# Short convolution's projections in a hybrid encoder trunk: the input projection by one level of Strassen in 12 pairs, the output projection in the down projection's form

## Chip, cores, metric

One core of one Trainium2 chip. The metric is the device time of one execution in microseconds (us), the median of several runs. The engines are TensorE (PE, with its weight loads shown as PEld), VectorE (DVE), ScalarE (ACT), GpSimd (POOL) and SyncE (SP), which here issues all DMAs.

## What is computed

Two layers on x of 1024 tokens by 1024 features, float32. Layer 0 is differential attention, layer 1 a gated short convolution; each is followed by a gated ConvFFN, and a last RMSNorm ends it. The part that changes is the mixer of layer 1:

```python
h = rms_norm(x, conv_norm_g)                       # 1024 x 1024
b, c, u = split(h @ w_in, 3)                       # w_in 1024 x 3072
x = x + (b * dwconv3(c * u, conv_w)) @ w_out       # w_out 1024 x 1024, taps over 3 tokens
```

Around it stand `x + conv_ffn(rms_norm(x))` of layers 0 and 1: an up projection 1024 x 5632, a convolution over 3 tokens, silu(gate) * val, a down projection 2816 x 1024.

## The kernel before

Everything is kept transposed: features on the 128 partitions, 1024 tokens along the free axis. X is 8 tiles of 128 x 1024. A float32 operand is split in a high part (`fp32r`, by ACT's copy) and a low part (the difference, by POOL for weights, by DVE for data), and each product is three matmuls: high x high, high x low, low x high. Every matmul has 512 columns. The instruction streams are written out by hand for each engine and tied by semaphores; each engine runs its own queue in order.

**Dense jobs.** `full_job` (and `down` in `ffn`) makes one 128 x 1024 output tile in a PSUM slot from one weight tile of up to 8 input tiles: 48 matmuls, or 42 where a down chunk has 7 tiles. A weight tile passes through SP (`load_tile`, which waits until the job two before has ended), ACT (`split_hi`) and POOL (`split_lo`); there are two buffers. The order of weight tiles is T_QKV, T_WO, T_D0 (down 0), T_CIN, T_COUT, T_D1.

**Strassen up stage (`ffn`, first half).** The FFN's up projection runs as 22 pairs of output tiles (gate and value). Its 2 x 2 blocks are: input features in two halves (even and odd tiles), tokens in two halves. One level in Winograd's form takes 7 block products in place of 8: `up_product` does 4 x 3 = 12 matmuls for each, 84 a pair. The sums of the weights are POOL's (`up_sums`), their high parts ACT's (`up_hi`), their low parts POOL's (`up_lo`). The sums of the data (XB, four sets of 28 KB) are made once per stage. ACT copies three products out of PSUM (`copied`), DVE adds the results together (`c11`, `c22`, `c12`, `c21`), multiplies by the norm's factor (`normed`), and convolves (`taps`). The weights of pair p + 2 are loaded when pair p has used its own.

**What makes the operands.** While the last dense stage before an up stage runs (`dense(l, base, n)`: attention's output projection, and the conv mixer's), each finished X tile is added (DVE `x_add`, L1360), stored to DRAM (SP), spread and split for the up stage (ACT `spread`, L1023 to L1039; DVE `operands`, L1335 to L1350), squared in place (ACT, L1043) and summed (POOL `square_add`, L1638). In the same jobs POOL makes pair 0's weight sums (L1596 to L1614) and low parts (L1632, `first_lo`). XB's last set overlaps the operands of the running jobs; `y_head` says that their tiles there have been read for the last time, which is two input tiles before the last job's end. Pair 1's weights are loaded after the last job.

**Down stage (`ffn`, second half).** 24 jobs: 3 chunks (8, 7, 7 hidden tiles) by 8 output tiles, each added to X. Jobs 0 and 1 start interleaved while the hidden tiles come back from DRAM: 3 tiles of job 0, 3 of job 1, then 5 and 5. In the last chunk of down 0 `add_and_norm` and `norm_act` make XGh and XGl, the split normalized input of the conv mixer (L1320, L346).

**The conv mixer.** `conv_pair`: 24 `full_job`s with T_CIN's weights on XGh, XGl, three for each of 8 feature tiles (c, u, b). DVE multiplies by the norm's factor, forms c * u, two taps, times b, and the low part; ACT the middle tap and the high part. The result lies in Yh, Yl on chip. Then `dense(1, T_COUT, 3)`: 8 jobs on Yh, Yl.

Of the kernel before, what the change touches and what calls it, by code (L numbers as in the profile page):

```python
# [26 lines left out]
P = 128  # L27
# [34 lines left out]
T_CIN = T_D0 + len(CHUNKS) * KT  # L62
T_COUT = T_CIN + 3 * KT
# [6 lines left out]
KP = KT // 2  # L70
DMA_SCRATCH = 1024
# [9 lines left out]
def build(nc, x_in, positions, weights, ups, params_in, consts_in, lams_in, out):  # L81
    ctx = ExitStack()
    with ctx:
# [72 lines left out]
        h_at = [144, 152, 160] + [8 * t for t in range(18)] + [144]  # L156
        Hs = [at(f"H{t}", [P, 2, S], AR + w * K, F32R) for t, w in enumerate(h_at)]
        Hf = [at(f"Hf{t}", [P, S], AR + w * K + 4 * K) for t, w in enumerate(h_at)]
# [51 lines left out]
        def gcol(norm, kt):  # L210
# [17 lines left out]
        G = [dict(cp=sem(f"g{l}_copied"), t=sem(f"g{l}_t_made")) for l in range(2)]  # L228
# [19 lines left out]
        c_free, cu_made, ct_mid, ct_made = sem("conv_mm_free"), sem("cu_made"), sem("ct_mid"), sem("ct_made")  # L248
        cy_made, cyh, cyl, c_pad = sem("cy_made"), sem("cyh_made"), sem("cyl_made"), sem("conv_pad")
# [3 lines left out]
        per_layer = {"a": 8 * FT, "b": 8 * FT, "sums": 4 * FT, "hi": 2 * FT, "lo": 2 * FT, "mm": 7 * FT, "out": 3 * FT,  # L253
                     "ev": 4 * FT, "rn": 2 * FT, "mid": 2 * FT, "tap": 4 * FT, "silu": FT, "h": FT, "st": 8 * FT, "pad": 1,
                     "hh": FT, "hl": FT, "add": 2 * KT}
# [56 lines left out]
        def square_sum(pe, n):  # L312

            src = X[:, 0, :] if n in (1, 3) else acc[:, :]
# [41 lines left out]
        def norm_factor(act, n):  # L356
# [3 lines left out]
            dst = FR if n in (1, 3) else R  # L360
# [9 lines left out]
        def conv_col(ft, c):  # L370
            return par[:, bass.ds(ft * 3 + (C_CONV + c), 1)]
# [33 lines left out]
        def nth(l, k, count):  # L405

            return l * per_layer[k] + count
# [4 lines left out]
        def _(sp):  # L412
# [113 lines left out]
            def up_a(l, p):  # L526
                f, s = F, p % 2
                sp.dma_start(U1f[s][:, 1, 0:4:3, :], ups[l * FT + p, :, 0:2, :]).then_inc(f[f"a{s}"], 16)

            def up_b(l, p):  # L530
                f, s = F, p % 2
                sp.dma_start(U2f[s][:, 1, 1:3, :], ups[l * FT + p, :, 2:4, :]).then_inc(f[f"b{s}"], 16)

            def dense(l, base, n):
                for kt in range(KT):
                    if (0 if l else 1) <= kt < KT - 2:
                        load_tile(sp, base + kt + 2, kt % 2)
                    sp.wait_ge(N[n]["x"], kt + 1)
                    sp.dma_start(x_dram[kt], X[:, kt, :]).then_inc(x_st[kt], 16)
                    if kt == 1:  # L540
                        up_a(l, 0)
                        up_b(l, 0)
                up_a(l, 1)
                up_b(l, 1)

            def h_load(l, t):
                sp.dma_start(Hf[t][:, :], h_dram[t]).then_inc(h_in[t % 8], 16)
# [4 lines left out]
            def h_store(l, p):  # L552
                f = F
                sp.wait_ge(f["h"], nth(l, "h", p + 1))
                sp.dma_start(h_dram[p], Tv[:, :]).then_inc(f[f"st{p % 2}"], 16)

            def ffn(l, base, n):
                f = F
                for p in range(FT):
                    if p + 2 < FT:  # L560
                        sp.wait_ge(f["mm"], nth(l, "mm", 7 * p + 4))
                        up_a(l, p + 2)
                    if p == FT - 1:
                        sp.wait_ge(f["mm"], nth(l, "mm", 7 * (FT - 2) + 7))
                        sp.wait_ge(f["st0"], nth(l, "st", 16))
                        sp.wait_ge(f["st1"], nth(l, "st", 16))
                        h_load(l, 0)
                        h_load(l, 1)
                        sp.wait_ge(f["st0"], nth(l, "st", 32))
                        h_load(l, 2)  # L570
                    if p:
                        h_store(l, p - 1)
                    sp.wait_ge(f["mm"], nth(l, "mm", 7 * p + 7))
                    if p + 2 < FT:
                        up_b(l, p + 2)
# [5 lines left out]
                sp.wait_ge(f["st0"], nth(l, "st", 16 * (FT // 2)))  # L581
                for t in range(3, CHUNKS[0][1]):
                    h_load(l, t)
                for j in range(len(CHUNKS) * KT):
                    c, m = divmod(j, KT)
                    n2 = base + j + 2
                    if n2 < T_END:
                        load_tile(sp, n2, n2 % 2, down_cols(n2))
                    if j == 0:
                        h_store(l, FT - 1)  # L590
                    if j == 1:
                        sp.wait_ge(f["st1"], nth(l, "st", 16 * (FT // 2)))
                        for kt in range(1, KT):
                            x_load(kt)
                    if c + 1 < len(CHUNKS) and m < CHUNKS[c + 1][1] - CHUNKS[c + 1][0]:
                        h_load(l, CHUNKS[c + 1][0] + m)

            dense(0, T_WO, 1)
            ffn(0, T_D0, 1)
            for n in range(T_CIN, T_COUT):  # L600
                load_tile(sp, n + 2, n % 2)
            dense(1, T_COUT, 3)
            ffn(1, T_D1, 3)
# [10 lines left out]
        def _(pe):  # L614
# [124 lines left out]
            def dense(d, base):  # L739
                def one_of(n):  # L740
                    wait(pe, N[1 + 2 * d]["x"], n - 1)
                    full_job(pe, n + base, n % 2, n % 2, Yh, Yl, (cyh, cyl) if n == 0 else None, n == KT - 1,
                             d == 0 and n == 2)
                if d == 0:
                    for a in range(2):
                        dense_ahead(a, (KT - 1,))
                else:
                    one_of(0)
                    one_of(1)
                for n in range(2, KT):  # L750
                    one_of(n)

            dense(0, T_WO)


            def up_weight(p, o, kp):

                s, c = p % 2, slice(kp * P, (kp + 1) * P)
                if o < 4:
                    return U1[s][:, 0, o, c], U1[s][:, 1, o, c]  # L760
                if p == 0:
                    return U2h_first[:, o - 4, c], U2l_first[:, c] if o == O_S3 else U2[0][:, 1, o - 4, c]
                return U2[s][:, 0, o - 4, c], U2[s][:, 1, o - 4, c]

            def up_product(p, o, kps):
# [3 lines left out]
                for kp in kps:  # L769
                    wh, wl = up_weight(p, o, kp)  # L770
# [7 lines left out]
            def ffn(l, base, n):  # L778
                f, g = F, G[l]

                def first_pair():
                    early = (0, 1, 2)
                    pe.wait_ge(f["lo"], nth(l, "lo", 1))
                    pe.wait_ge(N[n]["x"], KT - 1)
                    for kp in early:
                        pe.wait_ge(N[n]["lo"], 2 * kp + 2)
                        up_product(0, O_A11, (kp,))
                    up_product(0, O_S1, early)
                    up_product(0, O_A12, early)
                    pe.wait_ge(N[n]["lo"], 2 * KP - 1)  # L790
                    up_product(0, O_A11, (3,)).then_inc(f["mm"], 1)
                    up_product(0, O_S1, (3,)).then_inc(f["mm"], 1)
                    pe.wait_ge(f["out"], nth(l, "out", 1))
                    up_product(0, O_S2, early)
                    pe.wait_ge(N[n]["lo"], 2 * KP)
                    up_product(0, O_S2, (3,)).then_inc(f["mm"], 1)
                    up_product(0, O_A12, (3,)).then_inc(f["mm"], 1)
                    pe.wait_ge(N[n]["lo"], 2 * KP + 1)

                def half_pair(p):  # L800
                    pe.wait_ge(f["lo"], nth(l, "lo", 2 * p + 1))
                    if p == 1:
                        pe.wait_ge(N[n]["x"], KT)
                    wait(pe, f["ev"], nth(l, "ev", 4 * p - 4))
                    up_product(p, O_A11, range(KP)).then_inc(f["mm"], 1)
                    pe.wait_ge(f["ev"], nth(l, "ev", 4 * p - 1))
# [937 lines left out]
```

## Time and profile before

| | |
|---|---|
| time, median of 3 runs | 2413.07 us (2411.49 to 2415.57) |
| the profiled execution | 2413.57 us, its span 2411.8 us |
| PE / PEld busy | 97% / 79% |
| DVE / ACT / POOL busy | 56% / 39% / 43% |
| matmuls | 10404 |
| mean granted TensorE clock | 0.993 |
| DMA | 239.49 MB, mean 99 GB/s |

Rows of the trace read as: start in us from the span's start, duration in us, engine, source line, operation, destination<-sources, shapes, how many were merged, and in brackets the engine's idle time before it and what released it. Busy spans of matmuls overlap (each is shown with 0.39 us, while one starts every 0.23 us), so pace is read from starts and counts. "L292" and "L773 to L775" are the lines of the helpers in which dense and Strassen matmuls are issued. SPq rows are the times of issue; landing is told by its own line.

### The profile page before, as it was taken

The page shows a single profiled execution, that of the slowest core. Times are in us where ns is not written, and L with a number is a line of the kernel's source. Part 1 is how long each engine was busy: PE and PEld are TensorE (multiplying, and loading weights), DVE is VectorE, ACT ScalarE, POOL GpSimd, SP SyncE. Part 2 cuts the span into 40 slices and gives each one's busy share as a digit, 9 for nine tenths or more (in the row PEclk, how much of TensorE's full clock was granted, in tenths as well). Part 3 has the DMA queues.
Part 4 walks back from the last instruction along what each step waited for, and adds up shares of the span by engine and source line. Part 5 has one row for each costly group of instructions (what it writes and reads, how often), then busy time and mean ns, then how long its engine had stood idle before and what let it go on. Part 6 is the DMA issues. An engine that isn't in the chain of part 4 may idle for free.

```text
span 2411.8 us, 26211 instructions
## 1 busy us (share of the span) xinstructions
PE 2337.6 (97%) x10404; PEld 1906.8 (79%) x10404; DVE 1350.4 (56%) x1240; ACT 941.9 (39%) x1069; POOL 1025.6 (43%) x661
## 2 busy tenths in 40 slices
PE   8899989999999999999999999999999999999997
PEld 6688767777777888888888888888778888888886
DVE  7566699999365555556422233335555555563223
ACT  5112178888445444444212211113444444442112
POOL 1112113333467776674222412123776667732221
PEclk9999999999999999999999999999999999999999
DMA  3553374351322222223422111113222222234222
GB/s 129 171 175 116 134 198 120 91 140 51 107 96 70 84 92 79 87 79 131 175 90 72 48 53 44 52 43 105 79 86 81 87 80 79 80 130 174 90 80 93
DMA packets 73808, 239.49 MB, mean 99 GB/s; under 512 B 8160, under 2 KB 8544, under 8 KB 73696
## 3 DMA queue, kind: packets, MB, share of 16 engines
q1 hardware_dynamic: 73696, 237.95, 30.3%
q8 instruction: 76, 1.25, 0.2%
q14 instruction: 36, 0.29, 0.0%
HBM read 177.10 MB, written 60.82 MB: 99 GB/s over the span
## 4 chain that ended last, share of the span: by engine, by line
PE 75%; issue 14%; DVE 5%; POOL 3%; ACT 3%; DMA 0%; POOLq 0%; SPq 0%; DVEq 0%; ACTq 0%
PE PS L292 36%; PE PS L773 11%; PE PS L775 11%; PE PS L774 11%; DVE nb L1288 2%; POOL Wst L277 2%; PE PS L685 1%; PE PS L663 1%; PE PS L671 1%; PE PS L664 1%; DVE X L1307 1%; ACT X L969 1%; POOL X L1638 1%; ACT X L981 1%; ACT At L976 1%
## 5 line engine op out<-in xcount | busy, mean ns | idle before, releaser
L277 POOL TENSOR_TENSOR Wst<-Wraw,Wst 128x1024 fp32r<-128x1024 f32 (+1 forms) x111 | 263.3, 2373 | 875.2 <-ACT Wst L271 875.1
L773 PE MATMUL PS<-XB,U 128*128 128x512 f32 x1208 | 472.2, 391 | 6.9 <-POOL U L1632 6.7
L775 PE MATMUL PS<-XB,U 128*128 128x512 f32 x1224 | 477.8, 390 | 0.0
L774 PE MATMUL PS<-XB,U 128*128 128x512 f32 x1208 | 471.7, 391 | 0.0
L292 PE MATMUL PS<-H,Wst 128*128 128x512 f32 x2070 | 470.1, 389 | 0.6 <-POOL Wst L277 0.4
L292 PEld LDWEIGHTS PS<-H,Wst 128*128 128x128 f32 x2070 | 388.3, 188 | 82.1 <-DVE Tv L1425 0.8
L292 PE MATMUL PS<-XGh,Wst 128*128 128x512 f32 x1536 | 419.6, 394 | 23.5 <-POOL Wst L277 12.5
L271 ACT ACTIVATE Wst<-Wraw 128x1024 fp32r<-128x1024 f32 (+1 forms) x111 | 114.0, 1029 | 649.1 <-DMA Wraw<-weights 649.0
L292 PEld LDWEIGHTS PS<-XGh,Wst 128*128 128x128 f32 x1536 | 289.6, 189 | 87.0 <-issue 23.6
L773 PEld LDWEIGHTS PS<-XB,U 128*128 128x128 f32 x1208 | 227.8, 189 | 55.7 <-POOL U L1632 7.6
L775 PEld LDWEIGHTS PS<-XB,U 128*128 128x128 f32 x1224 | 230.8, 189 | 48.5
L774 PEld LDWEIGHTS PS<-XB,U 128*128 128x128 f32 x1208 | 227.7, 189 | 47.3
L292 PE MATMUL PS<-XGl,Wst 128*128 128x512 f32 x768 | 238.9, 392 | 0.0
L1632 POOL TENSOR_TENSOR U<-U1f,U 128x2048 fp32r<-128x2048 f32 x44 | 203.3, 4621 | 7.1 <-ACT U L1049 0.9
L1084 ACT ACTIVATE PS<-rawg,par 128x1024 f32<-128x1024 f32 x44 | 53.2, 1210 | 389.1 <-DVE rawg L1406 389.1
L292 PEld LDWEIGHTS PS<-XGl,Wst 128*128 128x128 f32 x768 | 145.9, 190 | 30.9
L1288 DVE TENSOR_REDUCE nb<-PS 128x1 f32<-128x1024 f32 x128 | 154.0, 1210 | 8.9 <-PE PS L664 8.9
L1429 DVE TENSOR_TENSOR H<-Hf,H 128x1024 fp32r<-128x1024 f32 x44 | 71.5, 1626 | 138.9 <-ACT H L1093 138.5
L1632 POOL TENSOR_TENSOR U<-U2f,U 128x1536 fp32r<-128x1536 f32 x42 | 149.2, 3553 | 0.0
L1596 POOL TENSOR_TENSOR U1f<-U2f 128x512 f32<-128x512 f32 x44 | 57.9, 1315 | 210.1 <-DMA U2f<-ups 210.1
L292 PE MATMUL PS<-Yh,Wst 128*128 128x512 f32 x480 | 130.4, 390 | 0.5 <-POOL Wst L277 0.4
L1417 DVE SCALAR_TENSOR_TENSOR PS<-rawg,par,PS 128x1024 f32<-128x1024 f32 x88 | 113.4, 1289 | 28.6 <-ACT PS L1084 27.1
(185 smaller groups left out, 3192.1 us busy)
## 6 DMA issues: line engine op xcount, KB each, us to landing
Wraw<-weights SPq DMA_DIRECT2D x79, 512.0 KB, 3.5
U1f<-ups SPq DMA_DIRECT2D x44, 512.0 KB, 4.6
U2f<-ups SPq DMA_DIRECT2D x44, 512.0 KB, 3.7
h_scratch<-Tv SPq DMA_DIRECT2D x44, 512.0 KB, 5.4
Hf<-h_scratch SPq DMA_DIRECT2D x44, 512.0 KB, 4.4
Wraw<-weights SPq DMA_DIRECT2D x32, 448.0 KB, 3.2
x_scratch<-X SPq DMA_DIRECT2D x16, 512.0 KB, 3.5
X<-x_scratch SPq DMA_DIRECT2D x16, 512.0 KB, 7.5
```

Source lines behind the costliest of these rows:

```text
L271: act.activation(w[:, 0, 0:cols], raw[:, 0:cols], ACT.Copy).then_inc(w_hi, 1)
L277: pool.tensor_tensor(w[:, 1, 0:cols], raw[:, 0:cols], w[:, 0, 0:cols].bitcast(F32), ALU.subtract).then_inc(w_lo, 1)
L292: ins = pe.matmul(ps[:, h * HALF:(h + 1) * HALF], w, m[:, h * HALF:(h + 1) * HALF], start=begin, stop=last and w is wl)
L773: pe.matmul(ps, wh, bh, start=begin, stop=False, skip_group_check=True)
L774: pe.matmul(ps, wh, bl, start=False, stop=False, skip_group_check=True)
L775: ins = pe.matmul(ps, wl, bh, start=False, stop=kp == KP - 1, skip_group_check=True)
L1084: act.activation(conv_ps(kind), src[:, 1:S + 1], ACT.Identity, bias=ffn_col(l, p, kind, 3), scale=ffn_col(l, p, kind, 1)).then_inc(f["mid" ...
L1288: dve.tensor_reduce(nb[:, b:b + 1], slot(c), axis=AX_X, op=ALU.min).then_inc(nb_done, 1)
L1417: dve.scalar_tensor_tensor(out=T, in0=raw[:, off:off + S], scalar=ffn_col(l, p, kind, c), in1=T, op0=ALU.mult, op1=ALU.add).then_inc(f["ta ...
L1429: dve.tensor_tensor(Hs[t][:, 1, :], Hf[t][:, :], Hs[t][:, 0, :].bitcast(F32), ALU.subtract).then_inc(f["hl"], 1)
L1596: pool.tensor_tensor(U1f[s][:, 1, O_S1, :], U2f[s][:, 1, 1, :], U2f[s][:, 1, 2, :], ALU.add).then_inc(f["sums"], 1)
L1632: pool.tensor_tensor(u[s][:, 1, :, :], uf[s][:, 1, :, :], u[s][:, 0, :, :].bitcast(F32), ALU.subtract).then_inc(f["lo"], 1)
```

## The change

- The input projection runs in the up stage's form: weights repacked on the host (`_conv_pairs`) in 12 pairs, for each two feature tiles the pairs (c, u), (c', u'), (b, b'). PE's `ffn` is split into `up(g)` and `down(g, base)`; g = 0, 1, 2 are the FFN of layer 0, the conv mixer, the FFN of layer 1. T_CIN, `conv_pair`, XGh/XGl for this norm and their jobs are gone.
- So the last chunk of down 0 (8 jobs of 42 matmuls) becomes a maker of operands: `dense(CONV)` on all engines, where `MADE_BY` = (T_WO, T_D0 + 16, T_COUT) is the first job. `y_head` comes after the third of 7 tiles in its last job.
- A conv pair's DVE work: evacuation and norm as in the FFN; then for (c, u) the product and two taps in PSUM, for (b, b') the two products y. y tiles 0 to 5 go to DRAM (`y_store`) and come back; tiles 6 and 7 stay in Tv and Tg.
- The output projection starts in the down stage's form: `conv_out` has jobs 0 and 1 interleaved as 3, 3, 3, 3, 2 and 2 tiles, then six jobs of 8 tiles in the order `y_last`; `y_head` comes after the fourth of 8 tiles in the last one.
- X passes through DRAM once more: stored in `dense(CONV)`, X0 loaded in pair 1, X1 to X7 loaded after `cyl` = 8. SP then enters `dense(2)`, whose first instruction is the load of T_COUT + 2.
- Buffers move (`h_at`, `y_at`, `u_set`), so that the sets in use don't overlap.

The core of the diff (in this order: constants, the new `conv` of SP, `conv_out` of PE, `conv` of DVE):

```diff
-T_CIN = T_D0 + len(CHUNKS) * KT
-T_COUT = T_CIN + 3 * KT
+T_COUT = T_D0 + len(CHUNKS) * KT
+CPAIRS = 3 * KT // 2
+PAIRS = (FT, CPAIRS, FT)
+MADE_BY = (T_WO, T_D0 + 2 * KT, T_COUT)
...
+            def conv():
+                for p in range(CPAIRS):
+                    if p + 2 < CPAIRS:
+                        up_next(CONV, p)
+                    if p == CPAIRS - 1:
+                        sp.wait_ge(F["mm"], nth(CONV, "mm", 7 * (CPAIRS - 2) + 7))
+                        for t in range(2):
+                            sp.wait_ge(cy_st[t], 16 * (KT // 2 - 1))
+                        for t in range(3):
+                            y_load(t)
+                    if p + 2 < CPAIRS:
+                        up_next_rest(CONV, p)
+                    if p and p % 3 == 0:
+                        y_store(p // 3 - 1)
...
+                sp.wait_ge(F["mm"], nth(CONV, "mm", 7 * CPAIRS))
+                for t in range(3, KT - 2):
+                    y_load(t)
+                sp.wait_ge(cyl, KT)
+                for kt in range(1, KT):
+                    x_load(kt)
...
+            def conv_out():
...
+                pe.wait_ge(w_lo, T_COUT + 1)
+                pe.wait_ge(F["ev"], nth(CONV, "ev", 4 * CPAIRS - 1))
+                job(0, (0, 1, 2), True, False)
+                pe.wait_ge(w_lo, T_COUT + 2)
+                pe.wait_ge(F["ev"], nth(CONV, "ev", 4 * CPAIRS))
+                job(1, (0, 1, 2), True, False)
+                job(0, (3, 4, 5), False, False)
+                job(1, (3, 4, 5), False, False)
+                job(0, (6, 7), False, True).then_inc(tile_done, 1)
+                job(1, (6, 7), False, True).then_inc(tile_done, 1)
+                for j in range(2, KT):
+                    pe.wait_ge(w_lo, T_COUT + j + 1)
+                    wait(pe, N[3]["x"], j - 3)
+                    job(j, y_last, True, True).then_inc(tile_done, 1)
...
+                def convolved(p):
+                    k = p // 3 * 2 + p % 3
+                    normed(g, p)
...
+                    dve.tensor_tensor(rawg[:, 1:S + 1], rawg[:, 1:S + 1], rawv[:, 1:S + 1], ALU.mult).then_inc(cu_made, 1)
+                    T = conv_ps(p % 3)
...
+                        dve.scalar_tensor_tensor(out=T, in0=rawg[:, off:off + S], scalar=conv_col(k, tap), in1=T,
+                                                 op0=ALU.mult, op1=ALU.add).then_inc(ct_made, 1)
...
+                outputs(CPAIRS - 1)
+                for t in range(3, KT):
+                    y_lo(t)
```

## Rows read from the trace of the kernel before

**Rows 1.** The page's first part: busy us, share of span, instructions.

```profile
PE 2337.6 (97%) x10404; PEld 1906.8 (79%) x10404; DVE 1350.4 (56%) x1240; ACT 941.9 (39%) x1069; POOL 1025.6 (43%) x661
```

**Rows 2.** Busy time by stage: up 0, input projection, up 1; its header names the columns.

```profile
core 0: us, PE busy (x) PEld busy (x) DVE busy (x) ACT busy (x) POOL busy (x), PEclk, DMA share, GB/s
707.50:1134.70 427.20, 423.13 (x1853) 348.51 (x1852) 245.85 (x250) 188.66 (x186) 290.33 (x131) 1.00 0.27 87
...
1376.30:1639.30 263.00, 263.00 (x1156) 217.07 (x1157) 96.84 (x65) 45.88 (x44) 60.86 (x25) 1.00 0.14 48
...
1726.50:2154.90 428.40, 424.37 (x1853) 349.38 (x1853) 245.60 (x250) 188.48 (x186) 290.37 (x131) 0.99 0.27 86
```

**Rows 3.** Timeline, down 0: the X adds behind two neighbouring jobs of 42 matmuls.

```profile
1260.77 1.22 DVE L1460 TENSOR_TENSOR X<-PS,X 128x1024 f32<-128x1024 f32 x1 [1.82 <-PE PS L292]
...
1270.29 1.23 DVE L1460 TENSOR_TENSOR X<-PS,X 128x1024 f32<-128x1024 f32 x1 [1.93 <-PE PS L292]
```

**Rows 4.** Timeline, PE's first matmuls of the input projection.

```profile
1376.29 0.73 PE L292 MATMUL PS<-XGh,Wst 128*128 128x512 f32 x2 [1.32 <-DVE X L1320]
```

**Rows 5.** Pair 1 of up 0 by timeline, then stretches at half clock by windows.

```profile
733.12 0.50 PE L773 MATMUL PS<-XB,U 128*128 128x512 f32 x1 [3.37 <-POOL U L1632]
...
734.10:737.40 3.30, 3.30 (x9) 2.53 (x9) 3.30 (x2) 1.21 (x1) 3.30 (x1) 0.50 0.00 0
...
1752.20:1758.00 5.80, 5.80 (x14) 4.54 (x15) 5.80 (x3) 1.54 (x2) 5.80 (x2) 0.50 0.00 0
```

**Rows 6.** Timeline, DVE at the end of the output projection.

```profile
1725.27 2.65 DVE L1341 TENSOR_TENSOR XBf<-XBf 128x512 f32<-128x512 f32 x2 [3.50 <-ACT XBf L1023]
1727.84 1.21 DVE L1360 TENSOR_TENSOR X<-PS,X 128x1024 f32<-128x1024 f32 x1
```

**Rows 7.** Timeline, DVE and POOL in the output projection's jobs; a narrower split in down 0.

```profile
1683.05 1.22 DVE L1360 TENSOR_TENSOR X<-PS,X 128x1024 f32<-128x1024 f32 x1 [2.74 <-PE PS L292]
...
1690.99 4.18 POOL L1638 TENSOR_TENSOR X<-X 128x1024 f32<-128x1024 f32 x1 [0.77 <-ACT X L1043]
...
1701.15 3.36 POOL L277 TENSOR_TENSOR Wst<-Wraw,Wst 128x1024 fp32r<-128x1024 f32 x1
...
1704.81 1.23 DVE L1360 TENSOR_TENSOR X<-PS,X 128x1024 f32<-128x1024 f32 x1 [2.54 <-PE PS L292]
...
1706.84 4.61 POOL L1632 TENSOR_TENSOR U<-U1f,U 128x2048 fp32r<-128x2048 f32 x1
...
1707.26 4.75 DVE L1347 TENSOR_TENSOR XBf<-XBf 128x512 f32<-128x512 f32 x1 [1.22 <-ACT XBf L1023]
...
1711.41 2.84 POOL L277 TENSOR_TENSOR Wst<-Wraw,Wst 128x1024 fp32r<-128x1024 f32 x1
...
1284.37 2.12 POOL L277 TENSOR_TENSOR Wst<-Wraw,Wst 128x896 fp32r<-128x896 f32 x1 [7.66 <-ACT Wst L271]
```

**Rows 8.** The seam into down 0: timeline, loads by tile, the page's median.

```profile
1142.62 1.06 ACT L1093 ACTIVATE H<-Hf 128x1024 fp32r<-128x1024 f32 x1 [1.55 <-DMA Hf<-h_scratch]
...
1154.53 2.40 POOL L277 TENSOR_TENSOR Wst<-Wraw,Wst 128x1024 fp32r<-128x1024 f32 x1 [33.93 <-ACT Wst L271]
...
1157.08 1.16 PE L292 MATMUL PS<-H,Wst 128*128 128x512 f32 x4 [0.44 <-POOL Wst L277]
...
L550 SPq DMA_DIRECT2D X<-x_scratch x7: 320/440/1455, 1159.3 to 1163.3; - x7
...
DMA to landing us min/median/max: 5.7/8.1/9.6
...
L264 SPq DMA_DIRECT2D Wraw<-weights x1: 333/333/333, 1168.2 to 1168.2; - x1
...
DMA to landing us min/median/max: 7.0/7.0/7.0
...
Wraw<-weights SPq DMA_DIRECT2D x79, 512.0 KB, 3.5
```

**Rows 9.** Timeline, up 0: DVE ends pair 1, ACT copies S2's sum in pair 2.

```profile
754.12 0.69 DVE L1402 TENSOR_TENSOR rawv<-PS,FR 128x512 f32<-128x512 f32 x1 [2.03 <-PE PS L775]
...
762.68 0.58 ACT L1012 ACTIVATE sP<-PS 128x512 f32<-128x512 f32 x1
```

More of the change, by code:

```diff
@@ L736, in _, with wo, up_weight @@
             run_steps(step, 15)
[L739 to L749, printed above, removed]
-                for n in range(2, KT):
[L751 to L758, printed above, removed]
+            def wo():
+                for a in range(2):
+                    dense_ahead(a, (KT - 1,))
+                for n in range(2, KT):
+                    pe.wait_ge(N[1]["x"], n - 1)
+                    full_job(pe, n + T_WO, n % 2, n % 2, Yh, Yl, None, n == KT - 1, n == 2)
+            wo()
+            def up_weight(g, p, o, kp):
+                s, c = u_set(g, p), slice(kp * P, (kp + 1) * P)
                 if o < 4:
@@ L850, in ffn, with job @@
                     if j < 20:
-                        wait(pe, f["add"], nth(l, "add", j - 3))
+                        wait(pe, f["add"], nth(g, "add", j - 3))
                     else:
-                        pe.wait_ge(N[n + 1]["x"], j - 19)
-                    if l and j == len(CHUNKS) * KT - 1:
+                        pe.wait_ge(N[g + 2]["x"], j - 19)
+                    if g and j == len(CHUNKS) * KT - 1:
                         last_down(j, range(*CHUNKS[-1]))
                     else:
-                        down(j, range(*CHUNKS[j // KT]), True, True).then_inc(tile_done, 1)
+                        job(j, range(*CHUNKS[j // KT]), True, True).then_inc(tile_done, 1)
+            def conv_out():
+                def job(j, tiles, first, last):
+                    s = (T_COUT + j) % 2
+                    for t in tiles:
+                        if j < 2:
+                            pe.wait_ge(cyl, t + 1)
+                        k = slice(t * P, (t + 1) * P)
+                        ins = products(pe, down_slot(j), Wst[s][:, 0, k], Wst[s][:, 1, k], Ys[t][0][:, :], Ys[t][1][:, :],
+                                       first and t == tiles[0], last and t == tiles[-1])
+                        if j == KT - 1 and t == y_last[3]:
+                            ins.then_inc(y_head, 1)
+                    return ins
+                pe.wait_ge(w_lo, T_COUT + 1)
[12 more added lines that the diff above has]
+                    job(j, y_last, True, True).then_inc(tile_done, 1)
             def square_half(half):
@@ L877, in last_down @@
                 square_half(1)
[L879 to L898 removed]
+            up(0)
+            down(0, T_D0)
+            up(CONV)
+            conv_out()
+            up(2)
+            down(2, T_D1)
         @block.scalar
@@ L1398, in c21 @@
[L1398 to L1407 removed]
+                ins.then_inc(F["pad"], 1)
@@ L1505, in last_add @@
+            dense(0)
+            ffn(0, T_D0)
+            dense(CONV)
+            conv()
+            dense(2)
+            ffn(2, T_D1)
             def last_add(half):
```

736 lines of the change are left out of this document (402 added, 334 removed).

## Prediction

> **What bounds the kernel now.** First the page's table of busy time: TensorE is busy 97% of a 2411.8 us span [rows 1], so what the change is worth is the matmuls it takes away, less the new idle time it opens in TensorE's queue. Second, the table by stage [rows 2]. The short convolution's input projection is one stretch, 1376.3 to 1639.3: 263.0 us in which PE never rests, at full clock. The FFN up stage, whose form it is to take, stands there twice: 427.2 and 428.4 us. Third, the pace: two X adds, each released by a down job of 42 matmuls, start 9.52 us apart [rows 3], so one matmul costs 0.2267 us from start to start, 48 of them 10.88 us and a pair of 84 of them 19.04 us. Last, the seams, by the timeline, since the projection gets three new ones: the down stage into it [rows 4, 6, 7], its own first two pairs [rows 5], and it into its output projection [rows 8].
>
> The profiled execution took 2413.57 us (1.8 us around its span), 0.5 us over the median of 2413.07; the sum is made against 2413.57.
>
> **1. The products.** Removed are 24 jobs of 48 matmuls, 1152 in all: 263.0 us [rows 2], plus the 1.3 us that PE waits for the last X tile before the first of them [rows 4]. Added are 12 pairs of 84, 1008 matmuls: 228.5 us. An up stage costs more than its matmuls: 22 pairs are 1848 matmuls, 418.9 us, so the excess is 8.3 us in the first [rows 2] and 9.5 us in the second. It is made of the norm's sum on PE, small waits in pair 0, and one large wait: pair 1 starts 3.4 us late, since its weight tiles can be loaded only when the job before has ended, and then comes a stretch at half clock [rows 5]. That stretch held 9 matmuls in 3.3 us in one stage and 14 in 5.8 us in the other; at full pace they take 2.0 and 3.2 us, so it cost 1.3 to 2.6 us. All this depends on the first two pairs, and the conv stage has the same code there, so it pays it once: I take the middle, 8.9 us. New stage 237.4 us, old 264.3: -26.9 us.
>
> The ten further pairs I cost at their matmuls alone. Their cover: DVE does less than in an FFN pair (one product and two taps in place of four taps and a gate), ACT less too, POOL the same. The tightest link is ACT's copy of S2's sum, which PE needs before the fifth product. In the FFN the pair that begins when c21 of the one before is read at 754.12 has it copied at 763.26 [rows 9], 9.3 us in, and needs it four products (10.9 us) in: slack 1.6 us. The queue ahead of it is shorter in the conv stage, so 0.
>
> **2. The last chunk of down 0 becomes the maker of the operands.** Its eight jobs now carry what the jobs of the output projection carry today: x_add, spread, the operand sums, squares, x stores, and on POOL the sums and the low parts of pair 0's weights. There a job lasts 10.88 us, here 9.52. Who pays is POOL's queue, since split_lo of the next weight tile stands in it. Measure from the end of job 3, whose X add starts at 1683.05 [rows 7]. POOL adds squares from 1690.99, makes four sums to 1701.15, and only then splits tile 6, to 1704.51: 21.5 us after that X add. Job 5's end, when tile 6 is needed, has its X add at 1704.81, 21.76 us after: a slack of next to nothing. In the new cadence the need comes at 19.04 us. The split is of 896 columns, 2.12 us instead of 2.40 [rows 7], which gives back 0.3. PE waits about 21.2 - 19.0 = 2.2 us. The next tile (1711.41 + 2.84, 31.2 us after, needed at 28.6 + 2.2 = 30.8, 0.3 to 0.6 less for the narrower splits) is then just in time. I take +2.2; bounds 0 (POOL's work moves with the jobs) and +5 (the second wait opens too). No clock loss is added: the wait of 1.3 us in [rows 4] was followed by none.
>
> DVE in that chain took 4.75 us for an operation of 128x512, a size that elsewhere takes it 0.69 [rows 9], while POOL ran 4.61 us of low parts [rows 7]. The Trainium skill, page "SBUF — State Buffer", section "Who interferes with whom", says that a DVE operation with two SBUF inputs and a GpSimd one that reads SBUF exclude each other, the loser waiting for the whole instruction. By that rule the tighter cadence could put one more DVE operation ahead of POOL's split; by the row of the two differences, 2.65 us [rows 6], this wait would then be 4.9 us and the sum 2398.8 us. The rows themselves carry 2.2; the bound of +5 holds the other.
>
> **3. The kt = 7 step of both later seams.** Tile 6's spread waits for y_head, which today comes 12 matmuls before the end of the last job; the change puts it 24 before. Today the add of X tile 7 starts at 1727.84, held behind DVE's two differences of tile 6 [rows 6], although PE was done at 1726.5 [rows 2]. With those differences earlier it can start at 1726.7. Everything to pair 1's weights hangs on it. So -1.1 us in the conv stage and -1.1 in the second FFN: -2.2 us. Bounds 0 and -2.2.
>
> **4. Into the output projection.** Before, PE passed from one to the other with no idle time. Now take the end of the last pair as zero. PE runs jobs 0 and 1 as 3, 3, 3, 3, 2, 2 tiles: job 0 ends at 84 matmuls = 19.0 us, job 1 at 21.8. Operand tiles 3 to 5 are loaded only after the last pair; in the down seam the third of these landed at 1142.6 [rows 8], 7.9 us after the pair's end at 1134.7 [rows 2]. Then ACT 1.06 [rows 8], DVE 1.22 as for an X add of that size [rows 7]: tile 5 is ready at 10.3, needed at 10.9, no wait. DVE's low parts of tiles 6 and 7 follow to 12.7. SP waits for exactly that (cyl = 8), and then issues seven X loads of 512 KB. Seven such loads landed 5.7 to 9.6 us after issue [rows 8], the first at 1165.0 and the last at 1172.8, so one behind another they come 1.3 us apart. Here the first lands near 16.2 (12.9 and the 3.5 us of a lone load, less 0.2), the seventh near 24.0.
> Behind them on SP's queue stands the load of weight tile 2, which waits for job 0's end: issued at 19.2, it lands behind the X loads at 25.3 (6.1 us later; the same tile behind X loads took 7.0 in the down seam, 3.5 is the median [rows 8]). ACT's split 1.06, POOL's 2.40, handovers 0.2: 29.0. PE has nothing from 21.8 on: 7.2 us idle. Who waits behind it: DVE, for job 2, and ACT's next spread behind the split; both catch up within the stage. The down seam hides the same chain since its job 1 has 30 matmuls left when the load goes out, and still waited 0.4 us [rows 8]; here 12 are left, 4.1 us less cover, and the X loads come earlier. The clock falls after such a wait; between 1.3 and 2.6 us [rows 5], I take 2.2, as the wait is longer. +9.4 us. Bounds: 4.6 + 1.3 = 5.9 if the load isn't held by the X loads; 13 if the low parts end 2 us later.
>
> **Sum.** -26.9 + 2.2 - 2.2 + 9.4 = -17.5 us: 2413.57 - 17.5 = **2396.1 us**.
>
> **Rivals.**
> A. The seams are covered: the weight load isn't held (5.9 in place of 9.4) and POOL follows its jobs (0 in place of 2.2). -26.9 - 2.2 + 5.9 = -23.2: 2390.4 us. For it: the transfers fill at most 0.27 of the DMA engines' time in these stages [rows 2]. Against: tile 6's split has no slack even today [rows 7].
> B. The chains pile up: 5 us in the last chunk, 13 at the output projection, nothing gained in part 3: -26.9 + 18 = -8.9: 2404.7 us.
> C. Slower than before. One mechanism: from pair 2 on the weight tiles land late, so POOL's sums, ACT's high part and, queued behind it, the copy of S2's sum come late in each pair. The slack is 1.6 us [rows 9]. The 17.5 us are used up over 10 pairs at 1.75 us each, that is when loads land 3.35 us later than in the FFN; at 4.5 us later the pairs cost +29 us: 2425.1 us. For it: SP's queue has new y stores in it. Against: they come after the next weight load in the queue, three times in the stage, while the FFN stores a tile in every pair.
> D. It does what it says and nothing else: 144 fewer matmuls, -32.6 us, 2381 us. The seams would have to be free, and those of [rows 5] aren't.
>
> **How the numbers follow.** Forecast 2396.1: 0.55. A: 0.20. B: 0.16. C: 0.05. D: 0.04. The likeliest case alone reaches from 2393 to 2399; for 8 in 10 the range takes in A and most of B: 2388 to 2404. A measurement can tell 0.2% (4.8 us) from no change. Faster by more than that means under 2408.7: all but C and a tail of B, 0.92; within it 0.03; slower 0.05.
>
> **What would show it.** By stage: the conv up stage near 236 us with about 1013 matmuls, one wait of PE on POOL's U near 3.4 us; one wait of PE on POOL's Wst of about 2 us before job 6 of down 0's last chunk; one of about 7 us before the third job of the output projection, its Wraw load landing about 6 us after issue, with a stretch at half clock behind it. Wrong would be: waits of PE inside pairs 2 to 11; no wait at the output projection; a last chunk that waits at every job.

## The result, and the profile after

The changed kernel takes 2399.84 us (median of 5 runs, 2398.33 to 2403.92), the kernel before 2413.97 us beside it (5 runs, 2411.49 to 2415.89). The ratio is 0.9944, with 95% between 0.9933 and 0.9955: faster by 13.5 us by the ratio and by 14.1 by the medians, where 17.5 were forecast (2396.1 us, range 2388 to 2404). The profiled execution took 2399.84 us with a span of 2398.0, against 2413.57 and 2411.8 before, so the traces have 13.8 us to explain.

The page of the changed kernel, its table of busy time, the clock by slices and the transfers. The row of rows 1 is answered by the first:

```profile
PE 2311.8 (96%) x10260; PEld 1884.2 (79%) x10260; DVE 1401.9 (58%) x1311; ACT 991.5 (41%) x1116; POOL 1138.8 (47%) x711
...
PEclk9999999999999999999999999999999999999998
...
U1f<-ups SPq DMA_DIRECT2D x56, 512.0 KB, 4.5
U2f<-ups SPq DMA_DIRECT2D x56, 512.0 KB, 3.8
Wraw<-weights SPq DMA_DIRECT2D x55, 512.0 KB, 4.1
...
X<-x_scratch SPq DMA_DIRECT2D x24, 512.0 KB, 7.3
```

There are 144 matmuls fewer than in [rows 1], as the diff says. The weight tiles of the dense jobs (Wraw) take a median of 4.1 us to land where they took 3.5 [rows 8], but the 24 of the old input projection are no longer among them. The pairs' weight tiles (U1f, U2f) take 4.5 and 3.8 us; before it was 4.6 and 3.7.

Where the time went is told by stage. Busy time of the changed kernel by stage: up 0, down 0, the input projection, its output projection; then four short stretches in which the granted clock was 0.50 (up 1 took 427.3 us):

```profile
core 0: us, PE busy (x) PEld busy (x) DVE busy (x) ACT busy (x) POOL busy (x), PEclk, DMA share, GB/s
709.10:1137.30 428.20, 424.12 (x1854) 349.38 (x1853) 245.39 (x250) 188.37 (x186) 290.01 (x131) 0.99 0.27 86
1137.30:1380.90 243.60, 241.48 (x1057) 199.21 (x1056) 105.98 (x73) 72.66 (x68) 79.63 (x35) 0.99 0.34 121
1380.90:1619.00 238.10, 234.06 (x1014) 191.81 (x1013) 107.46 (x113) 80.55 (x80) 160.36 (x71) 0.99 0.23 78
1619.00:1714.80 95.80, 89.38 (x385) 73.39 (x384) 56.90 (x41) 39.33 (x35) 46.18 (x19) 0.96 0.37 137
...
1361.50:1364.90 3.40, 3.40 (x10) 2.62 (x9) 3.40 (x2) 0.95 (x1) 3.40 (x2) 0.50 0.24 98
1647.40:1651.60 4.20, 4.20 (x10) 3.33 (x11) 2.98 (x4) 2.08 (x2) 0.00 (x0) 0.50 0.32 116
...
1405.90:1412.60 6.70, 6.07 (x14) 4.81 (x15) 6.67 (x3) 0.64 (x2) 6.67 (x3) 0.50 0.04 15
...
733.40:740.20 6.80, 5.54 (x13) 4.38 (x14) 6.80 (x4) 1.99 (x3) 6.80 (x3) 0.50 0.11 44
```

The input projection took 263.0 us [rows 2] and takes 238.1. The stages' starts and ends of before stand in [rows 2] too: up 0 went from 427.2 to 428.2, down 0 (1134.7 to 1376.3, 241.6 us) to 243.6, the output projection (1639.3 to 1726.5, 87.2 us) to 95.8, up 1 from 428.4 to 427.3. Up 0 starts 1.6 us later, at 709.1, although no line ahead of it has changed its work. What follows up 1 takes 1.0 us less. In all: +1.6 +1.0 +2.0 -24.9 +8.6 -1.1 -1.0 = -13.8 us.

What PE waited for in the changed kernel, from 640 us on, summed by releaser (total us, times, longest):

```profile
PE PS L306 <- POOL Wst L291: 11.2, 5, 6.4
PE PS L830 <- POOL U L1764: 10.1, 3, 3.4
PE PS L830 <- ACT sP L1088: 2.2, 4, 0.6
```

The U waits are the three second pairs, where there were two [rows 5]. Between 1410 and 1619, pairs 2 to 11 of the input projection, PE waits for nothing. The Wst waits lie one at each place where a weight tile is split late: the forecast's two are these, by PE's timeline (in brackets the idle time and its releaser):

```profile
1360.12 1.20 PE L306 MATMUL PS<-H,Wst 128*128 128x512 f32 x4 [1.81 <-POOL Wst L291]
...
1647.33 1.22 PE L306 MATMUL PS<-Y,Wst 128*128 128x512 f32 x2 [6.42 <-POOL Wst L291]
```

The bracket counts from the drawn end of the last matmul; by starts and pace the gaps are 2.0 and 6.6 us, which is how the forecast reckoned. The first stands before job 6 of down 0's last chunk, the second before the output projection's third job. A third, of 2.2 us near 687, is in attention's output projection, which the diff doesn't change and where before had none.

### The profile page after: what moved, and what is told of

Its sections match the earlier page's. It is cut to its first block, busy times and chain, and to the rows that moved or that the text cites. A ratio compares the mean times of both kernels' runs of the same rounds, so it can differ in the third digit from the quotient of the medians.

```text
span 2398.0 us, 26048 instructions
## 1 busy us (share of the span) xinstructions
PE 2311.8 (96%) x10260; PEld 1884.2 (79%) x10260; DVE 1401.9 (58%) x1311; ACT 991.5 (41%) x1116; POOL 1138.8 (47%) x711
## 4 chain that ended last, share of the span: by engine, by line
PE 72%; issue 14%; DVE 5%; POOL 5%; ACT 3%; DMA 1%; POOLq 0%; DVEq 0%; ACTq 0%
PE PS L306 24%; PE PS L830 14%; PE PS L831 14%; PE PS L832 14%; DVE nb L1393 2%; POOL Wst L291 2%; PE PS L749 1%; PE PS L727 1%; PE PS L735 1%; POOL X L1771 1%; PE PS L728 1%; DVE X L1412 1%; ACT X L1045 1%; DMA Wraw<-weights 1%; ACT X L1057 1%
## 5 line engine op out<-in xcount | busy, mean ns | idle before, releaser
L830 PE MATMUL PS<-XB,U 128*128 128x512 f32 x1532 | 599.8, 392 | 10.6 <-POOL U L1764 10.1
L832 PE MATMUL PS<-XB,U 128*128 128x512 f32 x1556 | 607.8, 391 | 0.0
L831 PE MATMUL PS<-XB,U 128*128 128x512 f32 x1532 | 598.6, 391 | 0.0
L291 POOL TENSOR_TENSOR Wst<-Wraw,Wst 128x1024 fp32r<-128x1024 f32 (+1 forms) x87 | 208.2, 2395 | 673.3 <-ACT Wst L285 673.3
L830 PEld LDWEIGHTS PS<-XB,U 128*128 128x128 f32 x1532 | 289.3, 189 | 73.2 <-POOL U L1764 11.4
L832 PEld LDWEIGHTS PS<-XB,U 128*128 128x128 f32 x1556 | 293.7, 189 | 61.6
L831 PEld LDWEIGHTS PS<-XB,U 128*128 128x128 f32 x1532 | 289.5, 189 | 60.0
L1764 POOL TENSOR_TENSOR U<-U1f,U 128x2048 fp32r<-128x2048 f32 x56 | 259.5, 4635 | 8.6 <-ACT U L1125 1.0
L306 PE MATMUL PS<-XGh,Wst 128*128 128x512 f32 x768 | 212.7, 396 | 22.5 <-POOL Wst L291 13.3
L1764 POOL TENSOR_TENSOR U<-U2f,U 128x1536 fp32r<-128x1536 f32 x53 | 188.7, 3560 | 0.0
L306 PEld LDWEIGHTS PS<-XGh,Wst 128*128 128x128 f32 x768 | 145.6, 191 | 54.4 <-issue 23.1
L1088 ACT ACTIVATE sP<-PS 128x512 f32<-128x512 f32 x168 | 98.3, 587 | 168.2 <-PE PS L832 168.2
L1125 ACT ACTIVATE U<-U1f 128x2048 fp32r<-128x2048 f32 x56 | 107.4, 1918 | 47.8 <-POOL U1f L1732 47.8
L306 PE MATMUL PS<-XGl,Wst 128*128 128x512 f32 x384 | 120.1, 394 | 0.0
```

The costliest lines, as they stand in the source:

```text
L291: pool.tensor_tensor(w[:, 1, 0:cols], raw[:, 0:cols], w[:, 0, 0:cols].bitcast(F32), ALU.subtract).then_inc(w_lo, 1)
L306: ins = pe.matmul(ps[:, h * HALF:(h + 1) * HALF], w, m[:, h * HALF:(h + 1) * HALF], start=begin, stop=last and w is wl)
L830: pe.matmul(ps, wh, bh, start=begin, stop=False, skip_group_check=True)
L831: pe.matmul(ps, wh, bl, start=False, stop=False, skip_group_check=True)
L832: ins = pe.matmul(ps, wl, bh, start=False, stop=kp == KP - 1, skip_group_check=True)
L1088: act.activation(dst[:, :], bank(p, role), ACT.Copy).then_inc(F["out"], 1)
```

## The experiments

Each is the changed kernel with one edit unless said otherwise. Ratios are to the kernel before, run beside it. The theory going in is the forecast's: every late microsecond sits at a seam, where POOL's or SP's queue delivers a weight tile late; the pairs themselves are free. The rivals were that the wait at the output projection comes from PE's order of jobs or from the clock alone, that POOL's wait moves with the jobs, and that the stages which cost more in unchanged code are slowed by the change.

**e1_xlate: the X loads out of the weight load's way.**

```
                 sp.wait_ge(cyl, KT)
-                for kt in range(1, KT):
-                    x_load(kt)
+                x_load(1)
...
                         load_tile(sp, base + kt + 2, kt % 2, down_cols(base + kt + 2))
+                    if g == 2 and kt == 0:
+                        for late in range(2, KT):
+                            x_load(late)
```

> Only the order of SP's queue changes: X1 is still loaded ahead, X2 to X7 after the output projection's weight tile 2. Theory (that load is held by the X loads ahead of it: 5.56 us to land): it lands in 3.6 us, PE's wait before job 2 falls from 6.4 to about 4.5 us, the kernel is 2 us faster than the changed one (about 2397.5 at its median). Rival (the wait is set by the late end of job 0 alone and the queue costs nothing): wait 6.4, no change. Rival 2: X2 to X7 land too late and job 3 waits instead: no gain.

Measured: 2399.23 us, ratio 0.9942 [0.9925, 0.9958]. The load of weight tile 2 in e1_xlate, its time to land (min/median/max), and PE's wait in the output projection:

```profile
DMA to landing us min/median/max: 3.6/3.6/3.6
...
PE PS L306 <- POOL Wst L291: 4.5, 1, 4.5
```

In the changed kernel the same load took 5.6 us, and the wait was 6.4. So 2.0 us of the wait were the seven X loads in front. The other 4.5 us are a lone load and two splits behind 12 matmuls. That is the lower bound the forecast had given (4.6). The stage gave back 1.1 us of them (94.7 us against 95.8): in e1_xlate 15 matmuls ran at half clock behind the wait, in 6.2 us, in place of 10 in 4.2, which costs 0.9 us more. The medians differ by 0.6 us, too little to tell from none, where 2 were expected.

**e2_order: more matmuls between the first job's end and the third's start.**

```
-                job(0, (3, 4, 5), False, False)
-                job(1, (3, 4, 5), False, False)
-                job(0, (6, 7), False, True).then_inc(tile_done, 1)
-                job(1, (6, 7), False, True).then_inc(tile_done, 1)
+                job(0, (3, 4, 5, 6, 7), False, True).then_inc(tile_done, 1)
+                job(1, (3, 4, 5, 6, 7), False, True).then_inc(tile_done, 1)
```

> Only the order of the first two output jobs changes: 3, 3, 5, 5 tiles in place of 3, 3, 3, 3, 2, 2, so that job 0 ends 4.1 us earlier and weight tile 2 is issued 4.1 us earlier. Theory: the seven X loads are still ahead of it in the queue and end at the same time, so the tile lands at the same place (some 24 us behind the last pair), takes about 9 us from issue, and PE waits 6 to 6.4 us as before: within 1 us of the changed kernel. Rival (cover is all that lacks): the wait falls to 2.3 us, 4 us faster plus the clock's 1.9.

Measured: 2400.35 us, ratio 0.9941 [0.9925, 0.9958]. The same load and wait in e2_order:

```profile
L278 SPq DMA_DIRECT2D Wraw<-weights x1: 333/333/333, 1632.8 to 1632.8; - x1
...
DMA to landing us min/median/max: 11.0/11.0/11.0
...
PE PS L306 <- POOL Wst L291: 7.8, 1, 7.8
```

The tile goes out sooner, right behind the seven X loads (issued from 1629.1 to 1632.1), and takes 11.0 us to land: PE's order alone gives nothing, because the load is then held longer. The wait was expected to stay at 6 to 6.4 us and grew to 7.8. Counted from the start of the stage the tile lands at 26.2 us, in the changed kernel at 24.8; 0.5 of this is that the X loads go out 0.5 us later, the rest has no cause found.

**e3_both: the two edits together.**

> Both of the former edits. Theory (two causes in series, each hidden by the other): tile 2 is issued at 15.2 us behind the last pair, lands at 18.8, is split by 22.4; PE waits under 1 us and the clock does not fall: 5.7 + 1.9 = 7.6 us faster than the changed kernel, about 2392 us, more than the sum of the two edits alone. If they add up only: 2 to 3 us. If the low parts of y tiles 6 and 7 are late, PE waits inside job 0 instead.

Measured: 2397.51 us, ratio 0.9932 [0.9915, 0.9948]. Its output projection by the table of stages, its waits there, and the load of weight tile 3:

```profile
1615.90:1708.90 93.00, 88.19 (x386) 71.74 (x385) 61.63 (x41) 39.28 (x35) 46.92 (x19) 1.00 0.39 141
...
PE PS L306 <- POOL Wst L291: 4.8, 4, 2.2
...
DMA to landing us min/median/max: 8.7/8.7/8.7
```

The stage falls by 2.8 us and the median by 2.3, not by 7.6. Tile 2 did as expected: it landed in 3.9 us, and PE waited 0.7 for it. But the one wait of 6.4 has become four of at most 2.2: the six X loads now stand before tile 3, which takes 8.7 us to land (PE waits 1.4 us), and before job 6 the split of its tile waits in POOL's queue (2.2 us), as in down 0. So moving one load hands the wait on to the next item of the queues; e7_best below, which spreads the X loads and moves POOL's sums too, takes most of it away. The stretch at half clock is gone (clock 1.00 over the stage).

**e4_sums: POOL's sums one job earlier.**

```
-                    if kt == 3:
+                    if kt == 2:
                         up_sums(g, 0, 0)
                         first_sums(g)
```

> One number changes: POOL makes the weight sums of pair 0 in job 2 of each of the three operand-making stages in place of job 3. Theory (POOL's queue holds back the split of weight tile 6): the waits of PE before job 6 vanish, about 2.0 us in the last chunk of down 0 with the 1.7 us of half clock behind it, and 2.4 us in the attention's output projection: 4 to 6 us faster than the changed kernel, about 2394 to 2396 us. Rival (the loads or ACT's part set that split): the waits stay. Rival 2 (the work is only moved): a wait of 1 to 2 us turns up before job 5 instead.

Measured: 2395.81 us, ratio 0.9926 [0.9909, 0.9943]. POOL in the last chunk of down 0 of the changed kernel, by timeline, shows what the edit moves:

```profile
1347.05 4.10 POOL L1771 TENSOR_TENSOR X<-X 128x1024 f32<-128x1024 f32 x1 [1.18 <-ACT X L1119]
...
1355.75 1.29 POOL L1746 TENSOR_TENSOR U2f<-U1f,U2f 128x512 f32<-128x512 f32 x1
1357.01 3.06 POOL L291 TENSOR_TENSOR Wst<-Wraw,Wst 128x896 fp32r<-128x896 f32 x1
```

Squares, four sums, and only then the split of tile 6, ended at 1360.07, 0.05 us before PE's job 6 starts. With the sums one job earlier PE waits nowhere between 1300 and 1372, and the stage of down 0 in e4_sums is:

```profile
1132.30:1372.60 240.30, 239.76 (x1058) 198.12 (x1057) 102.62 (x73) 72.07 (x67) 78.26 (x34) 1.00 0.35 123
```

3.3 us less than in the changed kernel: 2.0 of wait, and some 1.1 of the half clock that followed it (the row 1361.50:1364.90 above: 10 matmuls in 3.4 us, at 0.2267 us each 2.3). The median is 4.0 us under the changed kernel's, the low end of what was expected. The profiled execution was the fastest of the four (2390.16 us): it also had no stretch at half clock in up 0, behind the same 3.4 us wait. In attention's output projection there is no wait before job 6 and a new one of 0.9 us before job 5, so the second rival came true there in small.

**a_again: the changed kernel once more, unedited**, in the second group of runs.

> The changed kernel once more, unchanged, beside the next three on the same chip. Theory on its spread (the order in which DVE and POOL meet in the attention's output projection varies from run to run, and so does the length of the stretches at half clock): median 2398 to 2403 us; in its profile the wait before job 6 of that projection is either near 0.2 or near 2.4 us, with the same code.

Measured: 2399.79 us, ratio 0.9934 [0.9917, 0.9950]. Its profiled execution took 2396.0 us, 3.8 less than the first one, with the waits of the first: 2.2 us in attention's output projection, 3.4 before pair 1. In up 0 there is no stretch at half clock after that 3.4 us wait, where the first trace has 6.8 us of it, 5.5 of them with PE at work (the row 733.40:740.20); in the input projection 3.4 us of it stand in place of 6.8. By the matmuls in them that is 2.6 and 1.2 us. So 3.8 us differ between two executions of one kernel whose waits are the same.

**e5_actcopy: ACT's copy of a PSUM sum behind the high parts, not before them.**

```
                         act.wait_ge(N[n]["used"], KT - 4)
-                        copied(g, 0, 0, 1, sP1, 1)
                         act.wait_ge(G[g]["t"], 5 * i + 5)
                         act.activation(XB[i][:, 0, 4:7, :], XBf[i][:, 1, 4:7, :], ACT.Copy).then_inc(N[n]["hi"], 1)
+                        copied(g, 0, 0, 1, sP1, 1)
```

> In each operand-making stage ACT makes the last high parts of the data (kt = 7, operands 4 to 6) ahead of its copy of product 1, not behind it. Theory (that copy waits for PE and holds ACT's queue, so the earlier X add gained nothing): the wait of 0.8 us before pair 0's fifth product vanishes and pair 1's weights are ready 1.4 us earlier in all three seams: 3 to 4 us faster than the changed kernel, pair 1 still waiting 2.9 to 3.5 us. Rival (x stores or pair 1's loads set it): nothing moves.

Measured: 2390.69 us, ratio 0.9899 [0.9883, 0.9916]. ACT at the start of the input projection, first in the changed kernel:

```profile
1384.49 1.06 ACT L1111 ACTIVATE XB<-XBf 128x1024 fp32r<-128x1024 f32 x1 [0.96 <-DVE XBf L1452]
1387.96 0.60 ACT L1088 ACTIVATE sP<-PS 128x512 f32<-128x512 f32 x1 [2.41 <-PE PS L832]
1388.45 1.48 ACT L1115 ACTIVATE XB<-XBf 128x1536 fp32r<-128x1536 f32 x1
```

then in e5_actcopy:

```profile
1378.87 1.06 ACT L1111 ACTIVATE XB<-XBf 128x1024 fp32r<-128x1024 f32 x1 [0.98 <-DVE XBf L1452]
1380.13 1.49 ACT L1114 ACTIVATE XB<-XBf 128x1536 fp32r<-128x1536 f32 x1 [0.20 <-DVE XBf L1455]
1382.27 0.60 ACT L1088 ACTIVATE sP<-PS 128x512 f32<-128x512 f32 x1 [0.65 <-PE PS L832]
```

In the first, ACT stands idle 2.41 us for a PSUM sum that PE hasn't ended, and the high parts of three operand blocks, which need nothing from PE, queue behind. Turned round, the high parts start 0.2 us after the ones before, not 2.9 us after. PE's waits in e5_actcopy, from 640 us on:

```profile
PE PS L306 <- POOL Wst L291: 9.9, 4, 7.1
PE PS L830 <- POOL U L1764: 6.0, 3, 2.1
```

The waits for U fall from 3.4 to 2.0 each, and the four on ACT's copy (2.2 us in all) are gone, at all three seams. All waits together are 7.6 us less (26.0 to 18.4), of which 6.3 are the edit's; the rest is that the 2.2 us wait near 687 is not in this trace and that the one at the output projection is 0.7 longer. The time fell by 9.1 us (medians, against a_again), where 3 to 4 were expected; pair 1's wait, expected at 2.9 to 3.5 us, fell further. The two profiled executions differ by 6.9 us (2396.0 and 2389.15), about what the waits give. The rest of the 9.1 isn't settled; that stretches at half clock tend to be shorter behind 2.0 us than behind 3.4 is shown in the last section.

**e6_before_sums and e8_before_tuned: the same edits in the kernel before**, to learn how much of a gain belongs to the change. e6 has the sums in job 2, e8 has this and the turned copy.

```
-                    if kt == 3:
+                    if kt == 2:
                         up_sums(l, 0, 0)
...
-                        copied(l, 0, 0, 1, sP1, 1)
                         act.wait_ge(g["t"], 5 * i + 5)
                         act.activation(XB[i][:, 0, 4:7, :], XBf[i][:, 1, 4:7, :], ACT.Copy).then_inc(N[n]["hi"], 1)
+                        copied(l, 0, 0, 1, sP1, 1)
```

> The kernel before with POOL's weight sums in job 2 in place of job 3, in its two operand-making stages. It separates what the changed cadence costs from what was there before. Theory: there job 6 waits 0.2 us or, by the chance of the order on DVE and POOL, 2.4; the edit takes the chance away: 0 to 2.5 us faster than before (0 to 0.1%), against 4 us or more in the changed kernel, whose 9.5 us jobs turn the same queue into a sure wait.

> The kernel before with the two edits that apply to it too: sums in job 2 and ACT's copy behind the high parts. It tells how much of the best version's 39 us is the Strassen form's. Theory: its two seams gain 2 us each and the chance wait goes: 4 to 8 us faster than before, near 2407 us; so of the 39 us some 30 are the new form's with its own seams mended, close to the 32.6 us of the 144 matmuls. Rival (the edits act on the old form as much as on the new): 15 us or more.

Measured: e6 2411.20 us, ratio 0.9984 [0.9974, 0.9994] (10 runs, before at 2416.14 beside it); e8 2407.58 us, ratio 0.9962 [0.9947, 0.9977] (before at 2416.26). The edits are worth some 4 to 5 and 9 us in the kernel before, where 0 to 2.5 and 4 to 8 were expected. e6 gained more than the waits of before could give: they are 0.9 us on Wst after 640 us in the trace of before and 1.7 in that of e6. Its trace has one 3.4 us stretch at half clock where that of before has 6.8 (up 1), so part of the gain may be the clock's; this stays open.

**e7_best and e9_best_again: the seam edits together.** The changed kernel with the edits of e2, e4 and e5, and the X loads spread: X tile 1 ahead, 2 to 4 behind weight tile 2, 5 to 7 behind weight tile 3. e9 is the same kernel, in the group of e8.

```
+                    if g == 2 and kt < 2:
+                        for late in range(2 + 3 * kt, 5 + 3 * kt):
+                            x_load(late)
```

> All edits together: sums in job 2, ACT's copy behind the high parts, jobs 3, 3, 5, 5, weight tile 2 ahead of X2 to X4 and weight tile 3 ahead of X5 to X7, so that tile 3 is not held as it was in the former run with both seam edits (8.8 us to land, PE waited 1.6 us). Theory: the output projection stage falls from 95.8 to 88 us, the last chunk and the attention stage lose their waits, each seam 1.4 us: 8 + 6 + 4 = about 18 us less than the changed kernel's 2399.8, near 2383 us, 1.3% under the kernel before. Rival (what is freed in one queue is given back in the next, as tile 3 did): 2388 to 2392.

> The best version once more beside the tuned kernel before: 2376 to 2382 us, so that both stand against the same runs of before.

Measured: 2377.07 us, ratio 0.9833 [0.9816, 0.9849], and 2376.19 us, ratio 0.9837 [0.9819, 0.9854]. Down 0, input projection and output projection of e7_best, and its waits from 640 us on:

```profile
1133.70:1373.70 240.00, 239.67 (x1058) 198.23 (x1057) 103.20 (x73) 72.20 (x67) 78.41 (x34) 1.00 0.35 123
1373.70:1609.60 235.90, 232.69 (x1013) 190.95 (x1012) 109.41 (x114) 80.83 (x80) 161.64 (x72) 0.99 0.24 78
1609.60:1698.10 88.50, 87.37 (x386) 72.03 (x385) 57.65 (x41) 38.74 (x35) 48.72 (x19) 1.00 0.41 149
...
PE PS L832 <- POOL U L1764: 6.0, 3, 2.1
PE PS L306 <- POOL Wst L291: 2.8, 4, 1.1
PE PS L832 <- ACT sP L1088: 1.0, 1, 1.0
```

The longest wait for a weight tile is 1.1 us, and the output projection takes 88.5 us, 1.3 more than before the change. This version beats both kernels, by 37 to 40 us and by 23. Against e8, which has what the kernel before can use of the same edits, it is 31.4 us faster (2407.58 - 2376.19), near the 32.6 us that 144 matmuls cost at 0.2267 us. By the intervals of the two ratios the 31.4 is known to some 5 us. So the Strassen form itself gives nearly its full sum once its seams are covered, which was rival D's figure. The forecast for this version was 2383 us; it came out 6 us lower. The edits of e3, e4 and e5 gave 2.3, 4.0 and 9.1 us by themselves, and this version 23, which the spread X loads and the clock may explain; it wasn't taken apart further.

## Why the prediction was right or wrong

The time lies within the range, 3.7 us above the forecast. The mechanism of the two large terms, steps 1 and 4, held. Steps 2 and 3 each had one link wrong, and two differences of about 1 us the other way (the output projection, the stretch behind up 1) hide part of it.

**Step 1, the products: right.** Forecast 237.4 us for the stage less 1.1 of step 3, measured 238.1, with the 1014 matmuls (norm sums among them) and the one U wait of 3.4 us it named. Pairs 2 to 11 cost their matmuls and nothing else, so rival C's mechanism didn't occur: its weight tiles, loaded from 1430 us on, landed in a median of 3.8 us (U1f) and 3.8 (U2f), where in the FFN stages it is 4.6 and 3.7, far from the 3.35 us more at which C begins. The slack was read slightly low, 763.26 is 9.1 us behind 754.12 and not 9.3. The excess was mis-sized by 0.7: 9.6 us over 1008 matmuls (228.5), where 8.9 were taken from the FFN stages. The term in it that came out larger is the half clock: 14 matmuls in 6.07 us (the row 1405.90:1412.60) cost 2.9 us, where the middle of 1.3 and 2.6 was taken.

**Step 2, POOL's late split: the wait right, the clock wrong.** The wait was 2.0 us by starts where 2.2 were worked out from [rows 7]; e4_sums shows that it is POOL's queue. The step failed where it said "No clock loss is added". The clock did fall: from 1361.5 PE ran at 0.50 of its full clock (1.2 GHz) for 3.4 us, beginning 1.4 us behind the end of the 2.0 us wait, at a cost of 1.1 us. The same wait was followed by such a stretch in all six traces that have it, and e4_sums has neither. The 1.3 us wait of [rows 4] was no measure for a longer one.

**Step 3, the last step of the seams: wrong.** Its mechanism was followed one link too short. The X add did move up. DVE at the start of the input projection, changed kernel:

```profile
1381.11 1.23 DVE L1468 TENSOR_TENSOR X<-PS,X 128x1024 f32<-128x1024 f32 x1 [0.62 <-PE PS L306]
```

It starts 0.2 us after the last job's end at 1380.9, in place of 1.3 us after [rows 6]. But what hangs on it passes through ACT, and there the copy waits for PE: the 2.41 us of idle time shown under e5_actcopy took the gain, and pair 1's wait stayed 3.4 us as in [rows 5]. Up 1 did come out 1.1 us shorter, the very figure forecast, but that is luck: its wait is the same. In its stretch at half clock 7 matmuls ran in 3.1 us, which costs 1.5 us, in place of 14 in 5.8 [rows 5], which cost 2.6; that is the 1.1. As the last section shows, such a difference comes between executions of one kernel.

**Step 4, into the output projection: right.** Forecast 7.2 us of idle time and 2.2 of clock, 9.4; measured 6.6 by starts (6.4 in the bracket) and about 1.9 (the row 1647.40:1651.60: 10 matmuls in 4.2 us, 2.3 at full pace), and the stage 8.6 longer. The load landed 5.6 us after issue, not 6.1. e1_xlate split the wait as the step had, a lone load's part and a queued one's, and e3_both and e7_best showed the remedy that neither gives alone.

**Missed: stages whose code had not changed, +2.6 us.** 1.0 us is in up 0: behind the same wait 13 matmuls ran at half clock (the row 733.40:740.20) in place of 9 [rows 5], 1.3 us more of cost, and small differences take off 0.3. 1.6 us is in attention's output projection, a wait of 2.2 less the 0.6 by which the changed kernel was ahead until then. DVE and POOL there in the changed kernel:

```profile
667.23 2.54 POOL L291 TENSOR_TENSOR Wst<-Wraw,Wst 128x1024 fp32r<-128x1024 f32 x1 [1.10 <-ACT Wst L285]
...
667.43 2.89 DVE L1455 TENSOR_TENSOR XBf<-XBf 128x512 f32<-128x512 f32 x1
```

and in the kernel before:

```profile
668.02 2.97 POOL L277 TENSOR_TENSOR Wst<-Wraw,Wst 128x1024 fp32r<-128x1024 f32 x1 [1.29 <-ACT Wst L271]
668.03 0.68 DVE L1350 TENSOR_TENSOR XBf<-XBf 128x512 f32<-128x512 f32 x1
```

Where POOL starts 0.20 us ahead, DVE's operation of 128x512 takes 2.89 us and POOL's split 2.54. Where the two start within 0.01 us of each other, DVE's takes 0.68 and POOL's 2.97; in e2_order DVE starts 0.15 us ahead, with 0.69 and 2.80. What DVE ends late is handed on, by the timelines of the changed kernel and of before: ACT's high parts start at 670.35 and not at 668.75, POOL's squares at 673.73 and not at 672.12, POOL's split for job 6 at 683.70 and not at 682.10, and PE waits 2.2 us for it. The Trainium skill, page "SBUF — State Buffer", section "Who interferes with whom", tells of a DVE operation with two SBUF inputs and a GpSimd one that reads SBUF excluding each other; the trace agrees, 2.89 against 0.68 us. a_again and e1_xlate show this wait, e2_order and e3_both don't, with the same code in this stage. So it comes and goes with some tenths of a microsecond of timing, and it isn't shown that the change brings it. That the longer DVE operation causes the wait is read from the chain of rows, and was not tried by an edit.

The account of the missing 3.7 us, measured less forecast: unchanged stages +2.6, down 0 +1.1 (clock), input projection +1.8 (1.1 of step 3 and 0.7 of the excess), output projection -0.8, up 1 0.0, the stretch behind it -1.0, for which no cause was found.

## What to carry to other kernels

A stage that gets shorter keeps its price at the seams. Follow each seam through every in-order queue to PE (SP's loads, ACT's copies that wait on PSUM, POOL's splits), and count what stands ahead of the one item PE needs next. The cheapest mends were orders: sums one job earlier, an operation that needs nothing from PE before one that waits for it, bulk loads spread behind urgent ones; the mends at the output projection alone gave 0 to 2.3 us, those that act at three seams 4.0 and 9.1, all of them together 23 us. When a variant is judged, give the same mends to the old kernel too, since about 9 of the 40 us belonged to neither form.

## What the runs showed of the hardware that was not expected

The length of the half-clock stretch isn't set by the wait alone. Twelve traces have a wait of PE for U before pair 1, in two or three stages each, and in most of them the granted clock falls to 0.50 (1.2 GHz) shortly before or behind its end:

| wait for U before pair 1 | cases | no stretch | 3.4 us | 6.8 us |
|---|---|---|---|---|
| 3.4 us (before, after, a_again, e1, e2, e3, e4, e6) | 22 | 2 | 9 | 11 |
| 2.0 to 2.1 us (e5, e7, e8, e9) | 11 | 2 | 9 | 0 |

The lengths are those at which the granted clock was 0.50; the last part of a wait can lie within them (1.3 us of 6.8 in up 0 of the changed kernel). A wait of 2.2 us in attention's output projection was followed by no stretch in the three traces that have it (the changed kernel, a_again, e1_xlate), while the 2.0 us in down 0 was followed by 3.4 us each time. By 0.2267 us a matmul, a stretch before pair 1 costs 1 to 3 us. This is enough for the 3.8 us between the two traces of the changed kernel. So a microsecond or two in one stage of one trace is no sign of an edit's effect, and a shorter wait gains more than its own length only on the average. What decides between the lengths wasn't found.
